# Turning the merged row tiles in 32x32 blocks on VectorE and through DRAM, in a decoder trunk step

## What is computed

```python
def merge_branches(x, o_a, ga, o_b, gb, ma, mb, subln_g, lam_init, w_proj_a, w_proj_b, w_out):
    ...
    ya = (o_a.reshape(b, s, A_WIDTH) * jax.nn.silu(ga.astype(f32))).astype(x.dtype)
    yb = (o_b.reshape(b, s, B_WIDTH) * jax.nn.silu(gb.astype(f32))).astype(x.dtype)
    pa = jnp.einsum('bse,ed->bsd', ya, w_proj_a)
    pb = jnp.einsum('bse,ed->bsd', yb, w_proj_b)
    m = jax.nn.sigmoid(ma.astype(f32)) * pa + jax.nn.sigmoid(mb.astype(f32)) * pb
    return x + jnp.einsum('bsd,de->bse', m.astype(x.dtype), w_out).astype(x.dtype)
```

## Time and profile before

| | |
|---|---|
| time, median of 3 runs | 1668.65 us (1663.31 to 1669.62) |
| the profiled execution | 1665.28 us, its span 1663.3 us |
| TensorE busy | 1597.8 us, 96% of the span |
| VectorE, GpSimd, ScalarE busy | 756.8, 699.3, 564.3 us |
| mean granted TensorE clock | 0.993 of full speed |
| the projection loop | about 1442 to 1553 us |

### The profile page before, as it was taken

The page is one execution under the profiler, slowest core; times in us unless marked ns, Lnnn a source line. Parts: engine busy times, 40 slices in busy tenths (PEclk is TensorE's granted clock), DMA queues, the critical chain, the costliest instruction groups (busy, mean ns, idle before and its releaser), DMA issues.

```text
span 1663.3 us, 37301 instructions
## 1 busy us (share of the span) xinstructions
PE 1597.8 (96%) x14616; PEld 1371.4 (82%) x14616; DVE 756.8 (45%) x1852; ACT 564.3 (34%) x1341; POOL 699.3 (42%) x958
## 2 busy tenths in 40 slices
PE   7999999999999999999999999999899899999998
PEld 5787677878899999999999877778787788888787
DVE  5532576332473333733335554344454433588411
ACT  5311576121461213611135243343243334412300
POOL 5676330566534666446665122122121121666500
PEclk9999999999999999999999999999999999999999
DMA  5359896337873379933797899989888977865592
GB/s 173 101 151 192 268 308 224 97 94 154 275 258 91 91 161 270 302 100 108 167 291 238 283 309 303 329 280 308 297 290 296 330 246 232 285 199 173 194 330 95
DMA packets 351487, 369.84 MB, mean 222 GB/s; under 512 B 164113, under 2 KB 208274, under 8 KB 351314
## 3 DMA queue, kind: packets, MB, share of 16 engines
q1 hardware_dynamic: 306354, 308.55, 61.3%
q10 hardware_dynamic: 44960, 58.92, 10.6%
HBM read 310.83 MB, written 143.85 MB: 273 GB/s over the span
## 4 chain that ended last, share of the span: by engine, by line
PE 79%; DVE 4%; DMA 4%; POOL 4%; SPq 3%; issue 3%; ACT 3%; ACTq 0%; POOLq 0%; DVEq 0%
PE ps L2056 13%; PE ps L2058 13%; PE ps L2057 13%; PE ps L2211 4%; PE ps L2109 4%; PE ps L2268 4%; PE ps L2110 4%; PE ps L2111 4%; PE ps L2157 3%; PE ps L2231 3%; PE ps L2327 3%; PE ps L2218 2%; PE ps L2178 2%; POOL rs L1034 2%; PE ps L2310 2%
## 5 line engine op out<-in xcount | busy, mean ns | idle before, releaser
L1053 POOL TENSOR_TENSOR w_lo<-raw,w_hi 128x512 fp32r<-128x512 f32 x140 | 181.7, 1302 | 405.9 <-ACT w_hi L1263 405.4
L2056 PE MATMUL ps<-w_hi,hT 128*128 128x512 f32 x824 | 333.2, 404 | 2.2 <-POOL hT L1040 1.0
L2057 PE MATMUL ps<-w_lo,hT 128*128 128x512 f32 x824 | 329.6, 400 | 0.0
L2058 PE MATMUL ps<-w_hi,hT 128*128 128x512 f32 x824 | 329.6, 400 | 0.0
L2109 PE MATMUL ps<-w_hi,hT 128*128 128x256 f32 x768 | 222.9, 290 | 5.3 <-issue 5.0
L2056 PEld LDWEIGHTS ps<-w_hi,hT 128*128 128x128 f32 x824 | 206.1, 250 | 23.3 <-DVE w_lo L1569 1.8
L2058 PEld LDWEIGHTS ps<-w_hi,hT 128*128 128x128 f32 x824 | 205.9, 250 | 20.4
L2057 PEld LDWEIGHTS ps<-w_lo,hT 128*128 128x128 f32 x824 | 206.5, 251 | 19.2
L2110 PE MATMUL ps<-w_lo,hT 128*128 128x256 f32 x768 | 215.9, 281 | 0.0
L2111 PE MATMUL ps<-w_hi,hT 128*128 128x256 f32 x768 | 215.5, 281 | 0.0
L1107 POOL TENSOR_SCALAR qz<-qT,qcol 64x128 f32<-64x128 f32 x256 | 156.6, 612 | 111.6 <-PE ps L2157 54.6
(11 more groups left out here) (229 smaller groups left out, 2764.4 us busy)
## 6 DMA issues: line engine op xcount, KB each, us to landing
out<-in_cache_a_kv SPq DMA_DIRECT2D x32, 2040.0 KB, 13.6
k_in<-in_cache_b_kv SPq DMA_DIRECT2D x128, 256.0 KB, 4.1
v_in<-in_cache_b_kv SPq DMA_DIRECT2D x128, 256.0 KB, 6.4
raw<-in_w_in SPq DMA_DIRECT2D x104, 256.0 KB, 3.4
k_in<-in_cache_a_kv SPq DMA_DIRECT2D x104, 256.0 KB, 7.7
v_in<-in_cache_a_kv ACTq DMA_DIRECT2D x96, 256.0 KB, 6.1
out<-in_cache_a_kv SPq DMA_DIRECT2D x8, 2016.0 KB, 9.3
raw<-in_w_in ACTq DMA_DIRECT2D x40, 256.0 KB, 5.6
```

What stands on the lines that cost most here:

```text
L1053: pool.tensor_tensor(lo, raw_of(q), hi.bitcast(F32), ALU.subtract).then_inc(lo_done, 1)
L2056: pe.matmul(z, hi, wh, start=first, stop=False)
L2057: pe.matmul(z, hi, wl, start=False, stop=False)
L2058: return pe.matmul(z, lo, wh, start=False, stop=last)
```

## The change

Merged tiles 0 to 6 (`by_blocks(i)`, i < 7) are no longer turned on TensorE. VectorE turns each 32x32 block of the two `sig` halves in place (`m_turn`). SP stores them, in eight DMAs of 64 KB with runs of 128 bytes, to a DRAM scratch that has the columns as its rows, so that the blocks land in their turned places (`store_m`). SP then loads the turned tile into `hT[1]` (`load_m`). ScalarE copies it to `hT[0]`, and VectorE subtracts in place in `hT[1]`. Tiles 7 and 8 are still turned on TensorE. The high and low part of tile i are now made two rounds later (`move_m(i - 3)`, `m_low(i - 3)` in round i). `load_sig(0, i)` now waits for all stores of tile i - 2 to land (`m_sent`). The new semaphore values reuse semaphores that have another use earlier in the program.

```diff
+        m_turned_scr = dram("m_turned_scr", [D_MODEL, SEQ])
...
                 if i >= 2:
-                    sp.wait_ge(*((m_ready, 2 * i - 2) if br else (m_t, 2 * i - 2)))
+                    if br:
+                        sp.wait_ge(m_ready, 2 * i - 2)
+                    elif by_blocks(i - 2):
+                        sp.wait_ge(*m_sent(i - 2))
+                    else:
+                        sp.wait_ge(m_t, m_by_tensor(i - 2, 1))
...
+            def store_m(i):
+                sp.wait_ge(*m_turned(i))
+                for half in range(2):
+                    for blk in range(4):
+                        base = m_turned_scr[half * CW:half * CW + 1, i * P + 32 * blk:i * P + 32 * blk + 1]
+                        dst = bass.AP(base.tensor, base.offset, [[SEQ, 32], [32 * SEQ, CW // 32], [1, 32]])
+                        rows = sig[4 * (i % 2) + half][32 * blk:32 * blk + 32, :]
+                        sp.dma_start(dst, rows.rearrange("p (j r) -> p j r", r=32)).then_inc(m_sent(i)[0], 16)
+
+            def load_m(i):
+                sp.wait_ge(*m_sent(i))
+                sp.dma_start(hT[1][:, :, i * P:(i + 1) * P].bitcast(F32),
+                             m_turned_scr[:, i * P:(i + 1) * P].rearrange("(k p) r -> p k r", p=P))                    .then_inc(m_back(i)[0], 16)
...
             def move_m(i):
                 for half in range(2):
-                    act.wait_ge(m_t, 2 * i + half + 1)
+                    if by_blocks(i):
+                        act.wait_ge(*m_back(i))
+                        act.activation(hT_part(0, half, i), hT_part(1, half, i).bitcast(F32), ACT.Copy).then_inc(m_hi, 1)
+                        continue
...
+            def m_turn(i):
+                for half in range(2):
+                    dve.wait_ge(m_ready, 2 * i + half + 1)
+                    s = sig[4 * (i % 2) + half][:, :]
+                    dve.transpose(s, s).then_inc(m_turned(i)[0], 1)
...
-                if i:
+                if i and not by_blocks(i - 1):
                     turn_m(i - 1)
```

More of the change, by code:

```diff
@@ L570, in row_tiles, with by_blocks, m_turned, m_sent @@
             return enumerate((NT, *range(NT)) if kind == "v" else range(TILES))
+        def by_blocks(i):
+            return i < NT - 1
+        def m_turned(i):
+            return h_t, 2 * TILES + 2 * i + 2
+        def m_sent(i):
+            return sk_in[0][0], 16 * slot_uses(N_GROUPS - NKS, 0) + 128 * (i + 1)
+        def m_back(i):
+            s = 1 + i % 3
+            return sk_in[s][0], 16 * slot_uses(N_GROUPS - NKS + s, 0) + 16 * (i // 3 + 1)
+        def m_by_tensor(i, half):
+            return 2 * (i - (NT - 1)) + half + 1
         def z_done(u, at_, i):
@@ L988, in _ @@
                     load_y(1, i + 1)
+                if i >= 2 and by_blocks(i - 2):
+                    store_m(i - 2)
                 for br in range(2):
                     load_sig(br, i)
+                if i >= 2 and by_blocks(i - 2):
+                    load_m(i - 2)
             def load_xl(idx):
@@ L1444, in move_m @@
                 for half in range(2):
-                    act.wait_ge(m_t, 2 * i + half + 1)
+                    if by_blocks(i):
+                        act.wait_ge(*m_back(i))
+                        act.activation(hT_part(0, half, i), hT_part(1, half, i).bitcast(F32), ACT.Copy).then_inc(m_hi, 1)
+                        continue
+                    act.wait_ge(m_t, m_by_tensor(i, half))
                     act.activation(hT_part(0, half, i),
@@ L1537, in _ @@
                         split_hi(*divmod(q, KC))
-                if i:
-                    move_m(i - 1)
+                if i >= 3:
+                    move_m(i - 3)
             for q in range(Q_OUT + 4, Q_OUT + KC):
@@ L1542, in _ @@
             halves(NT, 1)
-            move_m(NT)
+            for i in range(NT - 2, TILES):
+                move_m(i)
             for idx in range(2 * TILES):
@@ L1855, in m_low @@
                     dve.wait_ge(m_hi, 2 * i + half + 1)
-                    dve.tensor_tensor(hT_part(1, half, i),
+                    dve.tensor_tensor(hT_part(1, half, i), hT_part(1, half, i).bitcast(F32) if by_blocks(i) else
                                       bank(6 + half).rearrange("p (c r) -> p c r", c=4)[:, :, 0:nrows(i)],
                                       hT_part(0, half, i).bitcast(F32), ALU.subtract).then_inc(m_lo, 1)
+            def m_turn(i):
[3 more added lines that the diff above has]
+                    dve.transpose(s, s).then_inc(m_turned(i)[0], 1)
             def gated(br, i):
@@ L1978, in _ @@
                     splits_of(range(Q_OUT + SPARE, Q_OUT + 4))
-                if i:
-                    m_low(i - 1)
+                if i and by_blocks(i - 1):
+                    m_turn(i - 1)
+                if i >= 3:
+                    m_low(i - 3)
             splits_of(range(Q_OUT + 4, Q_OUT + KC))
             gated(1, NT)
+            m_low(NT - 2)
+            m_low(NT - 1)
             for idx in range(2 * TILES):
@@ L2042, in turn_m @@
                     pe.wait_ge(m_ready, 2 * i + half + 1)
-                    if i:
+                    if i == NT:
                         pe.wait_ge(m_lo, 2 * i + half - 1)
```

## The result

| | before | after |
|---|---|---|
| median of the runs | 1669.13 us (1663.31 to 1670.08, 4 runs) | 1695.84 us (1691.37 to 1704.0, 4 runs) |
| ratio | | 1.0171, 95% interval 1.0143 to 1.0199 |
| profiled span | 1663.3 us | 1689.4 us |
| mean granted TensorE clock | 0.993 | 0.989 |

The change costs about 28 us. The prediction said 1685 with a range of 1672 to 1702: the sign and the range held. The forecast chain, however, was to cost at most 23 us, and the clock did what one of the rivals said.

The account below looks back on a forecast made before the run. TensorE was taken to bound the kernel, at 12.94 us a round. Loop +6.6, m_low +1.5 and end +8.6 summed to +16.7 us, added to a median of 1668.65: 1685 us, range 1672 to 1702.

Parts of the forecast that it names:

- The forecast chain: Main case over projection loop and its end: VectorE and the DRAM round trip slow it, +11 to +23 us, chance 0.52.
- one of the rivals: Projection loop: TensorE's idle time lowers its clock to half rate; +28 us if every round, +23 if some; chance 0.11.
- one of its own signs: Listed sign in the profile after that the forecast is wrong: the clock falls inside the projection loop.
- the end: After the projection loop: the last sig load waits for tile 6's stores (+7.7), low parts delay tile 8's turning (+0.9): +8.6 us.
- the loop: Projection loop: seven rounds +7.5, less 0.9 for the first round without a store, +6.6; m_low adds +1.5 us.
- crowded stores: Rival on SP's stores: a tile's 4096 runs crowd each other, 8.6 us; about +34 us, half way +25; chance 0.17.
- VectorE's sum: VectorE in each projection round: 12.4 us of work plus 1.2 for two transposes, 13.6 us against today's 12.94.
- The stores: SP, from m_turn to m_sent: eight issues 3.4 us plus landing 2.5, 5.9 us (bounds 4.6 and 9.0).
- The two-round loop: From the end of m_turn(i - 2) to m_turn(i), through stores, loads, GpSimd and VectorE: 27.9 us, 14.0 a round.
- The number of rounds: Projection loop: seven rounds at 14.0 us instead of 12.94, +1.1 each, +7.5 in all.
- m_low: VectorE's low part with two SBUF operands beside GpSimd's y_prepare_a: 0.25 us a round, six rounds, 1.5 us (bounds 0 and 1.0).

Follow-up runs that it names:

- f1: The changed kernel without its stores and loads, and with the low part of tiles 0 to 4 subtracted from a PSUM bank; ratio to before 1.0027.
- e1: The changed kernel without its DRAM stores and loads; sig loads wait only for VectorE's transposes, part of the output left out; ratio to before 1.0060.
- f3: The changed kernel with only load_m issued one round later, behind the next ogA loads; ratio to before 1.0163.
- g1: The changed kernel with a third set of sig buffers, load_m a round later, and the stores issued behind the sig loads; ratio to before 1.0051.
- e4: The changed kernel with m_low's first operand for tiles 0 to 4 read from a PSUM bank again (wrong values); ratio to before 1.0131.
- e3: The changed kernel with filler matmuls where TensorE waits for zyA, 24 in round 3 and 10 each in rounds 4 to 6; ratio to before 1.0128.
- g3: g1 with m_low of tiles 0 to 3 moved into VectorE's wait for GpSimd's rs in rounds 4 to 7; ratio to before 1.0040.

## Why the prediction was right, and where its sizes were off

The total is inside the range, but the forecast's own sum missed by 11 us, and by one of its own signs it was wrong: the clock fell inside the loop. By the traces the end is +9.2 for a forecast of +8.6, and the loop is +20.4 for a forecast of 6.6 + 1.5 = 8.1. So nearly the whole miss lies in the loop. That the total still fell in the range is owed to the room that was left for crowded stores and for the clock.

**VectorE's sum: right.** 13.6 us a round was worked out, 13.7 measured in three rounds of f1. With the rest of f1's end this makes the change a loss of 4.5 us by f1's ratio, before any DMA.

**The stores: right as a sum, by luck in its parts.** From the end of `m_turn` to the `sig` issue it is 1499.97 to 1505.64, 5.7 us, against 5.9. The eight issues took 4.15 us and not 3.4, and the landing behind them 1.5 and not 2.5. In round 3, where the issues took 7.35 us, the whole is 9.0 (1478.36 to 1487.38), the upper bound.

**The end: right.** +8.6 was predicted and +9.2 measured. `halves` starts 12.5 us after the last turning of `zyB` (1560.93 to 1573.45) where it was 4.2 (1544.00 to 1548.22): +8.3, against +7.7. In e1, without the stores and the wait for them, it starts 5.3 us after it, and the end is 21.7: stores and wait together are shown to be the cause. The low parts ahead of tile 8's turning fit the other 0.9, which no run took apart.

**The two-round loop: right in kind, too small in size, and not what set most rounds.** It was forecast at 14.0 us a round and takes 17.1. Its steps can be read off from one `m_turn` end (1499.97) to the one two rounds later (1534.24), 34.3 us:

- stores 5.7 (predicted 5.9), `sig` and `load_m` issues 2.3 (2.2),
- `ogA`, first issue to GpSimd's start: 8.2, **predicted 5.2**. This is the first term that failed. I took the duration of a transfer that found an empty queue. Now 1.5 MB of `sig` and `hT` stand right ahead of it: 2304 KB from the first `sig` issue (1505.64) to GpSimd's start (1516.15), in 10.5 us, is 225 GB/s. f3 and g1 show that it goes by the order: without `load_m` right ahead it is 6.3 to 6.8, and with the stores between the `sig` loads and `ogA` 4.7 to 5.9. The prediction named this load ahead of `ogA` as something in favour of the crowded rival, and didn't put it into its own sum.
- the rest, GpSimd's preparation, VectorE and the transposes: 18.1 (1516.15 to 1534.24), predicted 14.6. Of the 3.5, 1.6 are the clock: from the turning of `zyA` to that of `zyB` TensorE needs 7.64 us (1523.44 to 1531.08) and in f1 6.07 (1504.60 to 1510.67). The loop on record has no TensorE in it. The other 1.9 lie among GpSimd's and VectorE's operations that meet, such as L1878 with 1.63 us, and a slack of 0.7 where GpSimd is done before VectorE.

That slack is the point. The loop through DRAM holds VectorE up only in round 3, by 2.34 + 3.46 us. In rounds 4 to 6 a shorter loop of one round is the longer one, TensorE's and VectorE's, which the forecast doesn't have: VectorE waits for TensorE's `yT`, TensorE for VectorE's `zyA`. In f1 it takes 13.7, of which 7.64 from the turning of `zyB` to that of `zyA` and 6.07 back. In round 5 of after, `m_low` adds 1.06 (2.31 for 1.25), L1878 0.94 (1.63 for 0.69) and the half clock 1.57: 17.28, which is the round's length. Rounds 4 and 6 come out the same way (16.99 and 17.07).

**The number of rounds: wrong in both directions.** I gave seven rounds +1.1 us. In fact four rounds carry it all (21.6 and three of about 17, together +21.2), and the other two of the six are each 0.4 shorter than before. The first of the four is the longest: it holds VectorE's two waits for `ogA`, and behind the idle 6.26 us TensorE works longest at half clock.

**m_low: mis-sized.** 0.25 us a round was taken, with a bound of 1.0. Its two instructions went from a mean of 682 to 1268 ns, 1.17 us a round, in rounds 4 to 6. So more than the first of the pair meets GpSimd, which comes late enough to run beside both. In rounds 7 and 8 the pair takes 1.25 again. e4 and f1 show its worth: 3.3 and 3.5 us of loop against the predicted 1.5. The Trainium skill (SBUF — State Buffer, "Who interferes with whom") says that such an instruction contends with a GpSimd one that reads SBUF, and with one SBUF input doesn't. The runs agree on both: 1268 ns beside GpSimd with two SBUF operands, 664 with one (in f1 GpSimd's operations of 1.3 us run beside it).

**The clock: the rival I called unlikely came true as an addition.** The idle time was to come in two pieces of about 1 us. It comes in one, of 3.2 to 6.3 us, since all that delays VectorE stands ahead of `zyA`. The granted clock was 0.50 from 1488 to 1493, right behind the idle 6.26. From the turning of `zyA` to that of `zyB` it costs 2.3 us in round 3 and 1.6 in each of rounds 4 to 6, 7.0 in all; taking it away gives back 4.4 (e3), as the chain through DRAM then binds in part. The rival's total of +28 is what was measured, but by luck: it had seven rounds at 7 us of half clock. In rounds 4 to 6 the clock is low for about half of those 7 us.

**How it adds up.** By the ratios: f1 +4.5, with `m_low` +10 (e1), with the way through DRAM and the clock +28.5 (after). By the traces, the loop's 20.4 us are the 1.9 of f1, 3.6 for `m_low` (three pairs), 2.9 for L1878 (three times), 5.8 of waits for `ogA` in round 3 and 7.0 of clock, less 0.8 for the two short rounds. These are lengths on the path of one execution, and not what each would give back alone: the clock gives back 4 to 7 us (e3), and an `ogA` that comes about 2 us earlier gives 1.4 of loop (f3).

What stays open is why the end of g1, at 23.9, is still 2 us above that of e1. In g1 and g3, ScalarE waits 3.00 and 3.52 us there for a `w_out` load, and in e1 it has no such wait; that would fit stores in its way, but no run took it apart.

## What to carry to other kernels

Work moved from the bounding engine to one with half a microsecond to spare is paid for by the round, whatever the DMAs do: sum up the receiving engine first. For a wait that is put into an in-order queue, count not only the wait but the bytes that will then be released together, and look for who is last in that bunch; here a third set of buffers and the stores put between the burst and the urgent load (g1) took back two thirds of the whole loss. Ask which wait ends last on the path before you blame a late load: here `ogA` was 3 us late in every long round and held VectorE up in one of them. In the others it only moved GpSimd's work beside VectorE's. And when several bounds lie within a few per cent of each other, taking one away uncovers the next (e3, f3), while their effects on TensorE can meet in one idle piece, which here cost clock on top.

## What the runs showed of the hardware

- A store of 64 KB to DRAM in 512 runs of 128 bytes took a median of 0.51 us to issue and 2.0 us to land, eight of them 4.1 to 4.2 us on SP in a quiet stretch. In a crowded one they took 7.35.
- An idle time isn't a sure sign for the clock. In g1, the wait of 2.06 us before 1502.42 was followed by a granted clock of 0.51, and the longer one of 2.44 us before 1518.66 by 1.00. The busy times by stretch of g1:

```profile
1503.50:1507.00 3.50, 3.50 (x10) 2.69 (x9) 2.60 (x2) 0.21 (x1) 3.50 (x3) 0.51 0.88 234
1517.00:1521.00 4.00, 2.34 (x12) 2.00 (x13) 2.52 (x5) 0.60 (x1) 1.62 (x3) 1.00 0.61 137
```

- A VectorE instruction with two SBUF operands slows down GpSimd's work on tiny tiles as well: 128x4 operations went from 0.19 to 0.56 and from 1.01 to 1.33 us beside `m_low` in g3.
